# Gate tiles last and the rotation beside them in the second layers' mixer

## What is computed

```python
hn = rmsnorm(h, ln_mix[i])
(g_q, g_k, g_v, g_z, g_a, g_b, n_q, n_kc, n_vc, n_ks, n_vs, n_kw, n_vw, n_gate,
 s_q, s_k, s_v) = jnp.split(hn @ w_in[i], SPLIT_POINTS, axis=-1)
o_gdn = gated_deltanet(g_q, g_k, g_v, g_z, g_a, g_b, ...)   # 6 heads of 64; ends with rmsnorm(o) * silu(g_z)
o_nsa = native_sparse_attention(n_q, n_kc, ..., n_gate, positions, ...)   # begins with rope_2 of n_q, n_kc, n_ks, n_kw
o_sb = stick_breaking_attention(s_q, s_k, s_v)
```

## Time and profile before

| | us |
|---|---|
| median of three runs | 3872.31 |
| the profiled execution | 3872.61 |
| its span in the trace | 3870.7 |

### The profile page before, as it was taken

The page is one execution under the profiler, slowest core; times in us unless marked ns, Lnnn a source line. Parts: engine busy times, 40 slices in busy tenths (PEclk is TensorE's granted clock), DMA queues, the critical chain, the costliest instruction groups (busy, mean ns, idle before and its releaser), DMA issues. The chain is left out here.

```text
span 3870.7 us, 46526 instructions
## 1 busy us (share of the span) xinstructions
PE 3487.1 (90%) x19333; PEld 2710.6 (70%) x19333; DVE 1783.2 (46%) x2765; ACT 1306.7 (34%) x2030; POOL 423.0 (11%) x351
## 2 busy tenths in 40 slices
PE   5999897999998699998997978999989888699998
PEld 4877765888776568886775646788766665478885
DVE  4775465443333443333444444454454445345534
ACT  2332353222322432322412453333333134433423
POOL 0001000120001101100033000310001400012100
PEclk7989998999999899998998999999999989899999
DMA  6651215333211022222201012322121020223230
GB/s 230 203 163 44 77 33 192 120 112 109 98 66 54 27 105 90 103 89 64 76 7 46 12 33 82 98 88 99 66 86 50 2 56 1 93 65 99 98 109 22
DMA packets 230431, 316.17 MB, mean 82 GB/s; under 512 B 13117, under 2 KB 167590, under 8 KB 228942
## 3 DMA queue, kind: packets, MB, share of 16 engines
q1 hardware_dynamic: 230222, 313.20, 24.6%
HBM read 310.52 MB, written 6.85 MB: 82 GB/s over the span
## 5 line engine op out<-in xcount | busy, mean ns | idle before, releaser
L493 PE MATMUL out<-h_lo,w_hi 128*128 128x512 f32 x2608 | 1043.3, 400 | 43.6 <-DVE w_lo L484 39.3
L494 PE MATMUL out<-h_hi,w_hi 128*128 128x512 f32 x2608 | 1021.9, 392 | 0.0
L495 PE MATMUL out<-h_hi,w_lo 128*128 128x512 f32 x2608 | 1021.7, 392 | 0.0
L484 DVE TENSOR_TENSOR w_lo<-ring,w_hi 128x1024 fp32r<-128x1024 f32 (+2 forms) x461 | 562.7, 1227 | 986.1 <-ACT w_hi L479 981.3
L479 ACT ACTIVATE w_hi<-ring 128x1024 fp32r<-128x1024 f32 (+2 forms) x461 | 470.8, 1027 | 1160.7 <-PE out L495 1076.7
L493 PEld LDWEIGHTS out<-h_lo,w_hi 128*128 128x128 f32 x2608 | 493.7, 189 | 167.4 <-issue 50.3
L494 PEld LDWEIGHTS out<-h_hi,w_hi 128*128 128x128 f32 x2608 | 494.2, 189 | 112.3 <-issue 11.0
L495 PEld LDWEIGHTS out<-h_hi,w_lo 128*128 128x128 f32 x2608 | 493.5, 189 | 104.4
L493 PE MATMUL item_banks<-h_lo,w_hi 128*128 128x512 f32 (+1 forms) x632 | 290.4, 459 | 14.2 <-DVE w_lo L484 5.1
L494 PE MATMUL item_banks<-h_hi,w_hi 128*128 128x512 f32 (+1 forms) x632 | 255.7, 405 | 0.0
L495 PE MATMUL item_banks<-h_hi,w_lo 128*128 128x512 f32 (+1 forms) x632 | 254.6, 403 | 0.0
(11 more groups left out here) (498 smaller groups left out, 4651.6 us busy)
## 6 DMA issues: line engine op xcount, KB each, us to landing
ring<-in_mlp_w SPq DMA_DIRECT2D x30, 2048.0 KB, 8.5
ring<-in_w_up SPq DMA_DIRECT2D x44, 1024.0 KB, 7.0
tiles<-in_mod_w SPq DMA_DIRECT2D x80, 512.0 KB, 4.7
ring<-in_e_w_in SPq DMA_DIRECT2D x48, 512.0 KB, 4.2
ring<-in_w_down SPq DMA_DIRECT2D x10, 2048.0 KB, 7.8
ring<-in_w_in SPq DMA_DIRECT2D x16, 1024.0 KB, 5.2
ring<-in_o_w_in SPq DMA_DIRECT2D x7, 2048.0 KB, 7.9
tiles<-in_mod_w SPq DMA_DIRECT2D x8, 1024.0 KB, 8.7
```

Source lines behind the costliest of these rows:

```text
L484: return nc.vector.tensor_tensor(lo.bitcast(F32R), x, hi, ALU.subtract)
L493: nc.tensor.matmul(out, wh, xl, start=start, stop=False, **kw)
L494: nc.tensor.matmul(out, wh, xh, start=False, stop=False, **kw)
L495: return nc.tensor.matmul(out, wl, xh, start=False, stop=stop, **kw)
```

## The change

In the list of items the three gate tiles (`gz`) go from places 13 to 15 to the last three, 20 to 22, and the three query tiles and four key and value tiles move up by three places. The loads (`ranges`) are regrouped in the same order. `last_kv` is the count of items up to the last key tile and no longer that of all, and the rotation's lane begins 1.0 behind the end of that item (136.6 of planned time) and no longer behind the last (164.8). The waits of its first swap count the tiles that have left up to `last_kv`, so it doesn't wait for the gate tiles.

```diff
-        ranges += [[(W_GDN + t * 2 * P, 2 * P)] for t in range(2 * GDN_T)]
-        ranges += [[(W_NQ, 2 * P)], [(W_NQ + 2 * P, P), (W_KC, P)], [(W_KC + P, 2 * P)], [(W_KW, P)]]
+        ranges += [[(W_GDN + t * 2 * P, 2 * P)] for t in range(4)]
+        ranges += [[(W_GDN + 8 * P, P), (W_NQ, P)], [(W_NQ + P, 2 * P)], [(W_KC, 2 * P)], [(W_KC + 2 * P, P), (W_KW, P)]]
+        ranges += [[(W_GDN + 9 * P, 2 * P)], [(W_GDN + 11 * P, P)]]
         items = [Item("rows", 0, 0, 2 * P + 30, by_token[:, c:c + 1, :], (c,)) for c in range(TC)]
         items += [Item("conv", 1 + j // 2, j % 2 * P, P, qkv[:, j, :], tile=j) for j in range(3 * GDN_T)]
-        items += [Item("feat", 1 + j // 2, j % 2 * P, P, gz[:, j - 3 * GDN_T, :]) for j in range(3 * GDN_T, 4 * GDN_T)]
-        items += [Item("feat", 7 + j // 2, j % 2 * P, P, nq[:, j, :], scale=HD ** -0.5) for j in range(NSA_T)]
-        items += [Item("feat", 8, P, P, kv[:, 0, :]), Item("feat", 9, 0, P, kv[:, 1, :]), Item("feat", 9, P, P, kv[:, 2, :]),
-                  Item("feat", 10, 0, P, kv[:, 3, :])]
+        items += [Item("feat", 5 + (j + 1) // 2, (j + 1) % 2 * P, P, nq[:, j, :], scale=HD ** -0.5) for j in range(NSA_T)]
+        items += [Item("feat", 7 + j // 2, j % 2 * P, P, kv[:, j, :]) for j in range(4)]
         last_kv = len(items)
+        items += [Item("feat", 9 + j // 2, j % 2 * P, P, gz[:, j, :]) for j in range(GDN_T)]
...
-            rotary_lane(k, r, r.lane(at + 1.0, 28.0), [nq[:, j, :] for j in range(NSA_T)] + [kv[:, j, :] for j in (0, 2, 3)],
+            rotary_lane(k, r, r.lane(items[last_kv - 1].begin + items[last_kv - 1].length + 1.0, 28.0), [nq[:, j, :] for j in range(NSA_T)] + [kv[:, j, :] for j in (0, 2, 3)],
                         [kc2, vc2, ks2, kw2], kv_turned[:, 0:2, :], stat_banks, [(freed[0], (last_kv + 1) // 2), (freed[1], last_kv // 2)], [(normed, 2 * GDN_T)])
```

## The result

The changed kernel takes 3879.76 us (median of 20 runs, 3876.5 to 3885.4), the kernel before 3872.78 (20 runs, 3863.4 to 3878.2). The ratio, that of the means, is 1.0021 with a 95% interval of 1.0014 to 1.0028. The medians are 7.0 us apart (0.18%), the means 8.0 (0.21%): slower, at the edge of the 0.2% that the forecast counted as no change. The forecast was 3878.7.

The account below looks back on a forecast made before the run. TensorE was taken to bound the stretch beside items, the delta chain's latency the tail. Cost 9.6 less give-back 6.4 is +3.2 us a pass, twice +6.4 on 3872.3: 3878.7 us, range 3870.5 to 3886.5.

Parts of the forecast that it names:

- Beside the items: Stretch where TensorE is full with item products: rotation's ten matmuls, a filled wait and a stall cost 9.6 us a pass.
- The flipped step: VectorE's fourth rotation step comes ahead of the state update and waits for GpSimd, stalling TensorE at L3397 by 1.2 us.
- The tail: Delta chain after the last item, without rotation as filler: gives back 6.4 us a pass, bounds 4.5 to 8.4.
- Level to L3397: Tail, from a level's L3353 to the third round's second L3397: 15.6 us with rotation, 13.0 without, 2.6 gained.
- L3397 to L3532: Tail, from the second L3397 to the third round's last sum: 5.3 us with rotation, 3.3 without, 2.0 gained.
- the start of the fourth round: Tail, L3313 to L3332: 0.7 us gained from a turn matmul leaving, less 0.4 for a possible lower clock.
- Two levels behind it: Fourth round's next two levels lose two turn matmuls: 3.1 us to gain, 1.5 after 1.6 for the lower clock.
- lower bound of 4.5: Least give-back in the tail, us a pass: both clock losses whole and the turn matmul from L3313 to L3332 hidden anyway.
- within 0.2%: Forecast together with the case of coming out even (3871 to 3874): no measurable change, chance 0.56.
- Rival A: Lower clock in the tail and whole stall: cost 10.6, give-back 4.5, +6.1 us a pass, 3884.5; chance 0.36 above 3880.0.
- Rival C: TensorE has holes beside the items, a rotation matmul costs 0.2 us there: -4.0 us a pass, 3864.3; chance 0.08.
- rival D: First swap waits for VectorE's late copy of the last key tile, about 1 us a pass; no chance of its own.

Follow-up runs that it names:

- e4: Changed kernel with each of the rotation's six swap matmuls issued twice: 3883.59 us (one run).
- e1: Changed kernel with the rotation's lane 0.2 of planned time later, so VectorE's fourth rotation step stands behind the state update again: 3873.45 us, ratio 1.0007.
- e6: Kernel before with the rotation's lane 0.2 earlier, moving VectorE's fourth rotation step ahead of the state update in the tail: 3885.72 us (one run).
- e5: Changed kernel with the rotation 0.2 later, plus five unread matmuls in TensorE's waits in the tail: 3871.77 us, ratio 1.0000.
- e3: Changed kernel with the rotation left out whole, so queries and keys go unrotated: 3860.55 us, ratio 0.9973.
- e2: Kernel before with only the gate tiles last and the loads regrouped, the rotation starting at 164.8 as before: 3870.64 us, ratio 1.0002.
- e10: Changed kernel with rotation 0.2 later, low-part weight splits behind the first inverse, and four turn matmuls in the fourth round's wait: 3857.76 us, ratio 0.9963.
- e11: e10 with two unread matmuls more, before the third round's first L3397 and the fourth round's L3313: 3849.34 us, ratio 0.9943.
- e7: Kernel before with one low-part weight split in each of the first two rounds moved behind the first inverse: 3859.44 us, ratio 0.9965.

## Why the prediction was right, step by step

- *Beside the items.* Forecast 9.6 us a pass, measured 9.7. Its parts: the wait of 0.8 was filled; the stall was 1.3 for 1.2; so the ten matmuls cost 9.7 + 0.8 - 1.3 = 9.2, as forecast. The price of a matmul came from a row in like company (0.87 in the earlier trace rows), and e4 found its pitch again (0.86). The forecast took 0.2 off the stall for a shorter preparation by GpSimd; it was no shorter (3.67 us for 3.66), and the full 8.2 us from L3379 to L3397 came.
- *The flipped step.* Read from planned times alone, before any trace showed it. It was right in place, engine and size: e1 shows it by undoing it and e6 by making it where nothing else moved. The forecast called it a term of 1.2 us in a sum; it was over a third of the loss (2.6 of 7.0 us), and removing it takes one character.
- *The tail.* Forecast 6.4, measured 5.7. Level to L3397: 2.6 expected, 2054.53 to 2067.49 is 13.0 against 15.6, 2.6. L3397 to L3532: 2.0 and 2.0. **The term that failed is the start of the fourth round**: 0.7 to gain less 0.4 for the clock were forecast, and L3313 to L3332 takes 6.1 us in place of 4.5, a loss of 1.6, since all of it lay in the 10.2 us at 1.2 GHz. I had the loss of up to 1.5 as a bound and took a quarter of it; it came whole, and more. Two levels behind it gave 2.0 for 1.5 (8.5 to 6.5 us). And the end of the round, 2089.33 to 2105.43, took 16.1 us where it took 16.9 before, since the low clock that before lay over its last steps, from 2095.6, now began at 2104.5: 0.8 that I had not in the sum. So in the tail 1.9 us too much was offset by 0.5 and 0.8 too little; that the 5.7 came out so near to 6.4 is in part luck. The stated lower bound of 4.5 is also a slip: with both clock losses whole and nothing from the turn, the terms give 8.4 - 2.1 - 1.5 - 0.7 = 4.1.
- *The sum.* +3.2 forecast, +4.0 in the profile, twice; 6.4 against 7.0 in the medians. I gave 0.56 to "within 0.2%" and 0.36 to slower; the medians say 0.18% and the ratio 0.21%, so the result lies on the border and does not decide between the two. Rival A had the right cause for what was missing, the clock in the tail, and e5 puts it at up to 3.9 us a pass (50.6 in e3 to 46.7). Rival C falls by e4, rival D by the swap at 2006.86, the first, which waited for nothing. That items and loads are free is shown by e2. The clock alone does not make the loss: the item stretch is 9.7 us longer at a mean clock of 1.00.
- The page "TensorE: Matmul & The Clock Gate" of the Trainium skill says in its section "What's actually happening" that "the default state is throttled, and activity releases the throttle"; the forecast took from it that a tail without filler stays longer at the lower level. The trace agrees: 13.6 us at the lower clock in the tail, and in e5, where activity of no use keeps the clock up, a tail 3.9 us shorter than the one of e3 with nothing in its waits. But the give-back was 5.7, nearer to the 6.4 forecast than to the 4.5 that was taken to follow from the page.

## What to carry to other kernels

Work beside a full engine costs its own time, read from a row in like company; work spread evenly over a chain that waits is hidden only in part (here it cost 6.0 us, by e3), so place it at a wait (e10, e11). When a lane is moved in a schedule of planned times, compare the order of every queue before and after: a shift of 0.2 put one step ahead of a state update and made over a third of the loss. Look behind every wait for what the late engine did just before it: the largest gain here by one edit (e7) came from moving a split, one in each of two rounds, that stood in front of the step that all waited for.

## What the runs showed of the hardware

- The granted clock fell to 1.2 GHz not only behind waits of 3 us. In the changed kernel it fell at 2067.0 behind waits of 1 us and less in close sequence: TensorE had been busy for 4.5 us from 2060.2 to 2067.0, and the longest of its waits there was 1.0 us. The forecast had allowed for such a fall, at a quarter of its price.
- Once low it stayed so for 10.2 us in the changed kernel and in e10 with TensorE 8.5 and 8.8 us busy in them, and for 3.4 us in other places. The same chain thus costs 46.7 us (e5) to 50.6 us (e3). Two matmuls of 1 us each put into waits (e10 to e11) took 3.2 us off the tail.
- The same steps behind the same waits need not meet the same clock: the first round of the kernel before took 46.7 us at a mean of 0.96 in the first pass and 45.0 at 1.00 in the second. Two passes of one profile, with no edit between them, can thus differ by 1.7 us.
- A sum on VectorE (L3578) that took 0.69 us elsewhere took 1.24 us at 2019.54 while GpSimd's preparation ran; it costs nothing here, as VectorE was not the last.
